# A reordered router and a moved wait at the entry of a mixture-of-experts stage (float32, one core)

## The reference

```python
h = rms_norm_2(x, norm2_g)
coarse = softmax(h @ router_coarse)            # 4 groups, the best one is taken
fine = h @ router_fine                         # 32 experts; the best 2 of the 8 of that group
weights = softmax(best two) * coarse weight    # one weight per token and chosen expert
x = x + sum_e weights_e * ((silu(h @ w_gate[e]) * (h @ w_up[e])) @ w_down[e])
```

## Time and profile before

| | |
|---|---|
| median of 3 runs | 2104.69 us (2103.77 to 2108.5) |
| the profiled execution: its time | 2104.69 us |
| the profiled execution: its span, first to last instruction | 2102.9 us |
| busy: PE / PEld / DVE / ACT / POOL | 1915.1 / 1747.3 / 1426.7 / 1168.5 / 76.5 us |
| mean granted clock of PE | 0.961 of full speed |
| chain that ended last, by engine | PE 65%, DVE 22%, ACT 8% |
| router, fork and entry of the branch | about 1521 to 1557 us after the start |
| loop over the experts | from about 1557 us to the end |

### The profile page before, as it was taken

One profiled execution on the slowest core, in us unless ns is written; L12 is line 12 of the kernel. 1 busy time (PEld: TensorE's weight loads), 2 busy tenths in 40 slices (PEclk: granted clock), 3 DMA queues, 4 the chain that ended last, 5 costly groups with the idle time before them and its releaser, 6 DMA issues.

```text
span 2102.9 us, 30304 instructions
## 1 busy us (share of the span) xinstructions
PE 1915.1 (91%) x12946; PEld 1747.3 (83%) x12946; DVE 1426.7 (68%) x1425; ACT 1168.5 (56%) x1310; POOL 76.5 (4%) x94
## 2 busy tenths in 40 slices
PE   4999997988999889997997999897779999999997
PEld 3989997987998889997997999796668888888885
DVE  3686547545555677637645555755679999999995
ACT  2644344544444554333644444454368888888884
POOL 0000013000000000013000000000000000000000
PEclk9999998998999999999998999998879999999998
DMA  7333374524554333356542555332259999999993
GB/s 265 127 141 136 119 266 162 200 101 142 193 189 159 156 141 131 127 178 243 186 159 105 190 195 181 134 121 86 94 224 374 375 375 380 377 379 374 375 391 135
DMA packets 64524, 440.87 MB, mean 210 GB/s; under 512 B 7372, under 2 KB 7372, under 8 KB 14592
## 3 DMA queue, kind: packets, MB, share of 16 engines
q1 hardware_dynamic: 55296, 399.63, 50.6%
q0 software_dynamic: 8096, 35.30, 4.5%
q10 hardware_dynamic: 992, 3.93, 0.5%
HBM read 428.61 MB, written 10.23 MB: 209 GB/s over the span
## 4 chain that ended last, share of the span: by engine, by line
PE 65%; DVE 22%; ACT 8%; issue 2%; POOL 1%; DMA 1%; DVEq 0%; ACTq 0%; POOLq 0%
PE psum L188 64%; DVE ring_low L202 6%; ACT hl L198 3%; DVE arena L212 3%; DVE ht L202 2%; DVE rounded L202 2%; DVE rounded L212 2%; DVE arena L202 2%; ACT arena L198 1%; PE psum L192 1%; POOL arena L202 1%; DVE hl L202 1%; ACT rounded L198 1%; DVE arena L225 1%; DVE resid L202 1%
## 5 line engine op out<-in xcount | busy, mean ns | idle before, releaser
L202 DVE TENSOR_TENSOR hl<-ring,hl 128x2048 fp32r<-128x2048 f32 (+1 forms) x190 | 433.9, 2286 | 350.7 <-ACT hl L198 350.3
L188 PE MATMUL psum<-ht,hl 128*128 128x256 f32 x4992 | 630.2, 288 | 15.4 <-DVE hl L202 9.7
L188 PEld LDWEIGHTS psum<-ht,hl 128*128 128x128 f32 x4992 | 616.2, 195 | 25.1 <-DVE hl L202 10.3
L198 ACT ACTIVATE hl<-ring 128x2048 fp32r<-128x2048 f32 (+1 forms) x286 | 536.3, 1896 | 150.7 <-PE psum L188 122.9
L188 PE MATMUL psum<-hl,ax 128*128 128x512 f32 (+1 forms) x1608 | 351.9, 355 | 6.4 <-DVE ax L202 5.0
L198 ACT ACTIVATE arena<-psum 128x512 f32<-128x512 f32 (+5 forms) x232 | 121.0, 522 | 418.5 <-PE psum L188 405.5
L188 PEld LDWEIGHTS psum<-hl,ax 128*128 128x128 f32 x1608 | 264.8, 192 | 47.3 <-DVE ax L202 5.3
L202 DVE TENSOR_TENSOR ring_low<-ring,hl 128x2048 fp32r<-128x2048 f32 x96 | 215.3, 2285 | 19.3 <-ACT hl L198 19.1
L188 PE MATMUL psum<-arena 128*128 128x128 f32 (+6 forms) x1520 | 190.8, 291 | 30.1 <-ACT arena L198 23.5
L188 PEld LDWEIGHTS psum<-arena 128*128 128x128 f32 (+2 forms) x1520 | 174.7, 179 | 41.6 <-ACT arena L198 25.2
L188 PE MATMUL psum<-hl,ht 128*128 128x256 f32 (+1 forms) x1056 | 132.2, 287 | 26.8 <-DVE ht L212 24.0
(11 more groups left out here) (121 smaller groups left out, 1897.7 us busy)
## 6 DMA issues: line engine op xcount, KB each, us to landing
ring<-W SPq DMA_DIRECT2D x284, 1024.0 KB, 5.1
arena<-W SPq DMA_DIRECT2D x48, 1024.0 KB, 7.5
ht_raw<-W SPq DMA_DIRECT2D x46, 1024.0 KB, 7.8
gate_d<-arena POOLq DMA_DIRECT2D x32, 256.0 KB, 3.8
arena<-gate_d POOLq DMA_DIRECT2D x8, 1024.0 KB, 8.0
gn<-GB POOLq DMA_DIRECT2D x10, 512.0 KB, 4.1
arena<-GB POOLq DMA_DIRECT2D x6, 512.0 KB, 4.9
ring<-W SPq DMA_DIRECT2D x4, 512.0 KB, 4.5
```

The costliest lines, as they stand in the source:

```text
L188: return Nothing() if self.e is None else self.e.matmul(o, a, b, start=start, stop=stop, skip_group_check=skip_group_check)
L198: return self.e.activation(o, a, f, bias=bias, scale=scale)
L202: return Nothing() if self.e is None else self.e.tensor_tensor(o, a, b, op)
```

## The change

On PE: the logits of both token halves wait for the end of `norm_cut` (`V["n2"]`), no longer each for its half of `mo.hf`; the counts wait for `V["gw"]`, no longer for `V["mk"]`; `place` waits for `V["oh", g]`; and the first `gate_up(0, 0)` moves behind the wait for `SE` of expert 0 and `gather(1, 0)`. On ACT: the first `cut(2)` of the branch moves ahead of `place(0)`. On DVE: the four full copies `hf` move into `norm_cut`, each in front of its difference; the sum and reciprocal of the coarse softmax, with their wait for ACT's exponential, move up behind `coarse`; `mk` moves behind the wait for the fine exponential; the reduction and comparison that make the flag move ahead of `posm`; `prep` runs its loops in the other order and marks all four operations `oh`, so that whoever waits for `oh` waits for the fourth, where `gather` waited for the second before. No arithmetic changes.

```diff
--- before.py
+++ after.py
@@ -1125,12 +1125,12 @@
             norm(mo.n2.xn, "n2")
             rt = R("rt").rearrange("p (k n) -> p k n", k=8)
             b = bank("logits")
+            pe.wait_ge(s_dve, V["n2"])
             for t in range(2):
-                pe.wait_ge(s_dve, V["hf", t])
                 ins = mm(psum[:, b, 64 * t:64 * t + 36], [(mo.hf[:, k, 128 * t:128 * t + 128], rt[:, k, :]) for k in range(8)])
             ins.then_inc(s_pe, P("logits"))
             b = bank("counts")
-            pe.wait_ge(s_dve, V["mk"])
+            pe.wait_ge(s_dve, V["gw"])
             mm(psum[:, b, 0:32], [(C("s_lt_t"), mo.mk[:, 0, :])])
             mm(psum[:, b, 32:64], [(C("ones"), mo.mk[:, 0, :]), (C("s_lt_t"), mo.mk[:, 1, :])])
             mm(psum[:, b, 64:96], [(C("ones"), mo.mk[:, 0, :]), (C("ones"), mo.mk[:, 1, :])]).then_inc(s_pe, P("counts"))
@@ -1158,7 +1158,7 @@
 
                     g, i = divmod(e, 4)
                     b = beside + 1
-                    pe.wait_ge(s_dve, V["oh2", g])
+                    pe.wait_ge(s_dve, V["oh", g])
                     for t in range(2):
                         ins = pe.transpose(psum[:, b, 128 * t:128 * t + 128],
                                            mo.OH[g % 2][:, t, 128 * i:128 * i + 128].bitcast(F32), C("ident"))
@@ -1215,9 +1215,9 @@
                     gather(0, i, beside if i % 2 else into)
                 pe.wait_ge(s_act, A["x", 0, 3])
                 place(0)
-                gate_up(0, 0)
                 pe.wait_ge(s_act, A["SE", 0])
                 gather(1, 0, beside)
+                gate_up(0, 0)
                 gate_up(0, 1)
                 for e in range(32):
                     g, i = divmod(e + 5, 4)
@@ -1843,8 +1843,8 @@
 
                 for i in range(4):
                     gather(0, i, beside if i % 2 else into)
+                cut(2)
                 place(0)
-                cut(2)
                 gather(1, 0, beside)
                 cut(2)
                 gate_up(0)
@@ -2551,11 +2551,7 @@
 
 
             for t in range(2):
-                for j in range(2):
-                    ve.wait_ge(s_act, A["n2", "hi", t, j])
-                    copy(mo.hf[:, 4 * j:4 * j + 4, 128 * t:128 * t + 128], heads4(banks["n2", t, j]), "hf", t)
-            for t in range(2):
-                norm_cut(hTv, t, "n2")
+                norm_cut(hTv, t, "n2", full=mo.hf)
             unit()
             ve.wait_ge(s_act, A["xh"])
             lower(mo.XS, mo.n2.xn, "xl")
@@ -2568,6 +2564,9 @@
             red(col(0), lg[:, :, 0:4], MAX)
             tt(oh, lg[:, :, 0:4], wide(col(0), 4), ALU.is_equal)
             tt(lg[:, :, 0:4], lg[:, :, 0:4], wide(col(0), 4), SUB, "coarse")
+            ve.wait_ge(s_act, A["coarse"])
+            red(col(1), lg[:, :, 0:4], ADD)
+            rec(col(1), col(1))
             ts(oh, oh, -1.0, 1e30, ADD, MUL)
             for t in range(2):
                 tt(l3[:, t, :].rearrange("p (g e) -> p g e", g=4), lg[:, t, 4:36].rearrange("p (g e) -> p g e", g=4),
@@ -2577,12 +2576,9 @@
             stt(l3, oh1, -2e30, l3, MUL, ADD)
             red(col(3), l3, MAX)
             tt(gw, l3, wide(col(3), 32), ALU.is_equal)
-            tt(mk_, oh1, gw, ADD, "mk")
             tt(col(4), col(3), col(2), SUB, "fine")
-            ve.wait_ge(s_act, A["coarse"])
-            red(col(1), lg[:, :, 0:4], ADD)
-            rec(col(1), col(1))
             ve.wait_ge(s_act, A["fine"])
+            tt(mk_, oh1, gw, ADD)
             ts(col(5), col(4), 1.0, None, ADD, None)
             rec(col(5), col(5))
             stt(col(5), col(5), 0.5, col(1), MUL, MUL)
@@ -2592,12 +2588,12 @@
             tt(gw, gw, oh1, ADD, "gw")
             ve.wait_ge(s_pe, P["counts"])
             b = banks["counts",]
+            red(mo.flg[:, 0:1], psum[:, b, 64:96], MAX)
+            ts(mo.flag, mo.flg[:, 0:1], CAP + 0.5, None, ALU.is_gt, None, "flag")
             tt(posm, psum[:, b, 0:64].rearrange("p (t n) -> p t n", t=2), mk_, MUL)
             tt(posm, posm, mk_, ADD)
+            gone("counts")
             ts(posm, posm, -1.0, None, ADD, None, "posm")
-            red(mo.flg[:, 0:1], psum[:, b, 64:96], MAX)
-            gone("counts")
-            ts(mo.flag, mo.flg[:, 0:1], CAP + 0.5, None, ALU.is_gt, None, "flag")
 
             def few():
                 into, beside = 4, 6
@@ -2610,11 +2606,11 @@
                 def prep(g):
                     if g >= 2:
                         ve.wait_ge(s_pe, P["place", 4 * g - 5])
-                    for s in range(2):
-                        for t in range(2):
+                    for t in range(2):
+                        for s in range(2):
                             tt(mo.OH[g % 2][:, t, :].rearrange("p (e s n) -> p e s n", e=4, s=2)[:, :, s, :],
                                posm[:, t, 4 * g:4 * g + 4].unsqueeze(2).broadcast_to([128, 4, 64]),
-                               C("iota").unsqueeze(1).broadcast_to([128, 4, 64]), ALU.is_equal, ("oh", "oh2")[s], g, after=False)
+                               C("iota").unsqueeze(1).broadcast_to([128, 4, 64]), ALU.is_equal, "oh", g, after=False)
 
                 def turn_(e):
                     ve.wait_ge(s_act, A["sg", e])
```

## The result

The change makes the kernel slower: 2122.48 us (median of 8 runs, 2115.85 to 2128.05) against 2108.41 for the kernel before on the same chips (8 runs, 2103.69 to 2110.25); the ratio is 1.0064, with a 95% interval of 1.0051 to 1.0078, so 10.8 to 16.4 us more. The forecast was slower by 11.4 us, which lies in this interval; the forecast time, 2116.1 with a range up to 2119.5, missed. The profiled execution has a span of 2116.5, 13.6 more than the one before.

A forecast was written before the change was run, and what follows sets the result against it. The prediction took a chain of small dependent steps to bound the router and entry, and PE to pace the loop, so delays shift its end. Terms summed to +11.4 on 2104.69, giving 2116.1 us, range 2110.5 to 2119.5.

The forecast's parts named there:

- The logits: Router: PE starts the logits 3.98 us later, after all copies and differences; less 1.27 of slack, +2.7 us.
- The coarse wait and the fine one: Router softmax: DVE waits for ACT's coarse exponential behind a table load, +1.0 us, and for the fine one, +0.2.
- The counts: Router: PE's 2.35 us of counts no longer run beside DVE's work up to `gw`; +2.3 us.
- The flag: End of router: flag made 0.7 us earlier, but only DVE's last operation can run beside the branch; -0.2 us.
- `prep`: Before the first gather: PE waits for four operations of `prep`, two more than before; +0.7 us.
- The two moves: Branch entry: ACT's cuts delay `SE`, and PE makes both gate_ups only after `gather(1, 0)`; +3.0 us by order.
- The clock in the gap: Branch entry: PE's clock falls after idling 1.1 and 3.5 us around `place`; +1.7 us, bounds 0 and 3.4.
- The rival of the soaked-up delay: Expert loop: the weight stream, not PE, sets the loop's end, so no change, 2104.7 us; chance 0.06.
- the beat of 16.6: Expert loop: successive experts start 16.6 us apart, so a loop that starts x us later ends x later.
- the base of the sum: Whole kernel: time before the change taken as 2104.69 us, to which the +11.4 was added.
- the low stretch behind the first Silu: Early loop: clock 0.57 over 4 us, costing 1.7; a rival had it not come, 2112.7 us, chance 0.10.

The follow-up runs named there:

- experiment 7: Kernel before with only the later logits (full copies in `norm_cut`) and the counts waiting for `gw`; ratio 1.0028 (1.0017 to 1.0039).
- experiment 8: Kernel before with ACT's first `cut(2)` moved to the start of the branch and later cuts one place ahead; ratio 0.9970 (0.9960 to 0.9980).

## Why the prediction was right and wrong

- *The logits*: forecast +2.7, measured +2.70 (also alone, experiment 7). The cover of 1.3 that DVE's two `lo` operations gave was used up and the rest was paid.
- *The coarse wait and the fine one*: +1.2 forecast. From the first reduction to the end of `gw` it took 5.09 before and 1541.38 - 1535.21 = 6.17 after: +1.1. The exponential started 0.02 behind the table load (1535.25 + 1.28, then 1536.55), so what the Trainium skill adds for a drain ("ScalarE: Activation LUTs", What ACT_TABLE_LOAD costs) did not come here either.
- *The counts*: +2.3, measured 2.44 - 0.12 = +2.3, also alone.
- *The flag*: -0.2; 1543.82 to 1545.77 is 1.95, where it was 2.16.
- *`prep`*: +0.7; PE started 1.58 behind the first operation and not 0.91.
- *The two moves*: +3.0, measured 2.9 with the gap filled. That ACT's alone is free, and PE's alone costs 1.6 and not 3.0, was not in the prediction.
- *The clock in the gap*: +1.7, measured 1.9.
- *The rival of the soaked-up delay* fell: the loads moved with PE (1554.51 to 1567.84), and the loop kept its beat.
- *Two slips in the prediction's text.* The rows of ACT at 1599.40 and 1616.03 are the Silu of experts 2 and 3, not a copy; the beat of 16.6 is the same. The low end of the range adds up to 2110.9 (2112.7 less 1.8), not 2110.5, and the high end to 2118.8 before the "little for the clock"; neither changes that 2122.48 lies above it.

Two steps failed. The first is the base of the sum, "2104.69, which is also the median": three runs were taken for the time of the kernel. The 8 runs beside the change, these three among them, have a median of 2108.41, 3.7 higher; over the 29 runs of the kernel before beside experiment 8 they lie between 2103.7 and 2112.6, with a median of 2109.1. Ahead of the router alone the same instructions take 1520.4 to 1528.4. 2108.41 + 11.4 would have been 2119.8. The range was made of the change's bounds alone and held nothing for this spread, which is as large as they are. The second is the clock in the loop, for which the sum has no term. I took the low stretch behind the first Silu as a thing that stays, or, in a rival, goes away; it became longer, 0.58 over 8 us where the kernel before has 0.57 over 4:

```profile
1584.00:1592.00 8.00, 7.39 (x20) 5.83 (x21) 7.66 (x4) 5.66 (x5) 0.00 (x0) 0.58 0.61 231
```

S0-S1 is 17.6 in all three profiles with both moves and the gap left open, 16.4 in both of the kernel before. 11.4 + 1.25 = 12.7, or 0.60%, against a measured 0.64% (0.51 to 0.78). Of the 6.4 us by which the forecast time was short, 3.7 are the base and 1.25 the first turn; the other 1.4 are within the interval of the ratio. Why the stretch is longer there is not shown: filling the gap takes it away, so it hangs on what PE did before, but the other kernels have 15.9 to 17.5 at that place, and two of those with 15.9 have 18.2 in the next turn. The terms of the sum came out within 0.2 each, by the waits that were forecast. That they make 11.4 to the tenth is luck, since one is 0.1 too high where another is 0.2 too low, and the clock's 1.7 was taken over from another place in the loop.

## What to carry to other kernels

A wait that is moved to a later mark costs the work that it stops overlapping, less the slack of the other input: look for which of two inputs comes last, and by how much. In two lists written by hand for two engines, a move in one can be free, a move in the other cheap, and the pair dear (here 0, 1.6 and 4.7 us): check them together, and put helpers' work (here the splitting of weights) where its engine idles ahead of the chain. A change of a few microseconds in a kernel of two thousand should be read between two rows of the trace, since the whole moves by more than that from run to run; and an absolute time needs a range for the base as well.

## What was not expected of the hardware

- The start of the router, with the same instructions ahead of it, moved by 8 us in 1520 over the kernels, and by 5.7 in one kernel, with a granted clock of 0.97 or 0.95 over the same 400 us.
- After idle times of 1.11 and 0.63 us around a short `place` the clock was at the half level in one kernel (0.50 over 1550 to 1553); after 1.1 us alone it stayed at 1.00 in the kernel before (1546 to 1552).
- 14 matmuls more, whose results are never read, in a wait took 3.7 us off the entry and the first turn (1.94 + 1.74).
